# Stick-breaking attention: both heads of a chunk in one instruction on ScalarE, VectorE and GpSimd, and the diagonal closed in the scores

## What is computed

```python
z = jnp.einsum("bhtd,bhsd->bhts", qb, kb) * scale
causal = s_idx < t_idx
log_not = jnp.where(causal, jax.nn.log_sigmoid(-z), 0.0)
tail = lax.cumsum(log_not, axis=3, reverse=True) - log_not
log_a = jax.nn.log_sigmoid(z) + tail
a = jnp.where(causal, jnp.exp(log_a), 0.0)
outs.append(jnp.einsum("bhts,bhsd->bhtd", a, vb))
```

## Time and profile before

| | before |
|---|---|
| median of 3 runs | 2425.4 us (2420.01 to 2426.77) |
| the profiled execution's own time | 2425.43 us |
| its span, first to last instruction | 2423.6 us |
| PE busy | 2293.8 us, 95% |
| DVE, ACT, POOL busy | 959.4, 843.0, 975.7 us |
| granted TensorE clock, mean | 0.955 of full speed |

### The profile page before, as it was taken

One profiled execution on the slowest core, in us unless ns is written; L12 is line 12 of the kernel. 1 busy time (PEld: TensorE's weight loads), 2 busy tenths in 40 slices (PEclk: granted clock), 3 DMA queues, 4 the chain that ended last, 5 costly groups with the idle time before them and its releaser, 6 DMA issues.

```text
span 2423.6 us, 28293 instructions
## 1 busy us (share of the span) xinstructions
PE 2293.8 (95%) x10366; PEld 1801.5 (74%) x10366; DVE 959.4 (40%) x1433; ACT 843.0 (35%) x1410; POOL 975.7 (40%) x435
## 2 busy tenths in 40 slices
PE   7999999998889899999997999999999879999997
PEld 5888887775446688888784888888877547888886
DVE  3121347257663511244754321134523652212245
ACT  4222235325652422223523332222433752322222
POOL 4444444551002544444552354444344313444442
PEclk9999999999888999999997999999998879999999
DMA  4222222331001223223231132222231001322221
GB/s 162 104 92 99 104 104 87 122 121 36 1 1 52 85 89 104 87 104 107 85 111 45 70 105 103 93 97 103 70 104 70 1 1 70 104 88 102 97 93 70
DMA packets 29801, 202.67 MB, mean 84 GB/s; under 512 B 3360, under 2 KB 4000, under 8 KB 6048
## 3 DMA queue, kind: packets, MB, share of 16 engines
q1 hardware_dynamic: 28800, 198.55, 23.3%
q10 hardware_dynamic: 928, 3.14, 0.4%
HBM read 198.54 MB, written 2.10 MB: 83 GB/s over the span
## 4 chain that ended last, share of the span: by engine, by line
PE 86%; DVE 6%; ACT 4%; issue 2%; POOL 1%; DMA 1%; ACTq 0%; SPq 0%; DVEq 0%; POOLq 0%
PE PS L879 26%; PE PS L881 26%; PE PS L880 26%; PE PS L1185 2%; PE PS L1154 2%; PE PS L1113 1%; DVE NMAX L1558 1%; PE PS L1286 1%; DVE ACC L1344 1%; PE PS L1274 1%; ACT PT L677 1%; DVE TMP L1424 1%; PE PS L948 1%; DMA RAW<-wstream 1%; POOL X L437 1%
## 5 line engine op out<-in xcount | busy, mean ns | idle before, releaser
L412 POOL TENSOR_TENSOR WL<-RAW,WH 128x1024 fp32r<-128x1024 f32 x368 | 909.5, 2474 | 1335.3 <-ACT WH L478 1335.3
L879 PE MATMUL PS<-XH,WH 128*128 128x512 f32 (+1 forms) x2200 | 867.6, 394 | 29.9 <-DVE XL L1336 23.3
L880 PE MATMUL PS<-XL,WH 128*128 128x512 f32 (+1 forms) x2200 | 856.6, 389 | 0.0
L881 PE MATMUL PS<-XH,WL 128*128 128x512 f32 (+1 forms) x2200 | 856.1, 389 | 0.0
L478 ACT ACTIVATE WH<-RAW 128x1024 fp32r<-128x1024 f32 x368 | 388.6, 1060 | 1293.1 <-PE PS L881 1255.4
L879 PEld LDWEIGHTS PS<-XH,WH 128*128 128x128 f32 x2200 | 417.7, 190 | 126.1 <-issue 26.7
L880 PEld LDWEIGHTS PS<-XL,WH 128*128 128x128 f32 x2200 | 417.8, 190 | 87.9 <-issue 4.1
L881 PEld LDWEIGHTS PS<-XH,WL 128*128 128x128 f32 x2200 | 417.5, 190 | 85.7
L879 PE MATMUL PS<-HH,WH 128*128 128x512 f32 x672 | 261.4, 389 | 0.0
L880 PE MATMUL PS<-HL,WH 128*128 128x512 f32 x672 | 261.4, 389 | 0.0
L881 PE MATMUL PS<-HH,WL 128*128 128x512 f32 x672 | 261.4, 389 | 0.0
(11 more groups left out here) (193 smaller groups left out, 1667.5 us busy)
## 6 DMA issues: line engine op xcount, KB each, us to landing
RAW<-wstream SPq DMA_DIRECT2D x183, 1024.0 KB, 4.8
X<-xT SPq DMA_DIRECT2D x4, 512.0 KB, 9.6
WORK<-memT ACTq DMA_DIRECT2D x2, 1024.0 KB, 5.3
outT<-WORK SPq DMA_DIRECT2D x8, 256.0 KB, 2.1
RAW<-wstream SPq DMA_DIRECT2D x2, 512.0 KB, 6.8
PB<-WORK ACTq DMA_DIRECT2D x8, 127.8 KB, 2.4
CST<-consts SPq DMA_DIRECT2D x1, 912.0 KB, 11.6
WORK<-constsb SPq DMA_DIRECT2D x1, 256.0 KB, 13.2
```

The source lines that it names most:

```text
L412: pool.tensor_tensor(WL[:, s, :, :].rearrange("p a b -> p (a b)"), RAW[:, s, :], WH[:, s, :, :].rearrange("p a b -> p (a b)").bitcast(F), ...
L879: pe.matmul(o, wh, xh, start=start, stop=False)
L880: pe.matmul(o, wh, xl, start=False, stop=False)
L881: return pe.matmul(o, wl, xh, start=False, stop=stop)
```

## The change

Steps become pairs: `SBPAIRS` lists 24 of (chunk, key tile), and each operation of ACT, DVE and POOL takes both heads of a pair in one instruction, over a tile of two rows. The lags are 2 and 3, in pairs. The slots are grouped in twos; L goes to one of two slots of a pair (half of PB, and a new tile LT). The diagonal's bf16 matmul moves from the end of the tail to behind the scores, ahead of clip; DVE's mask multiplication is gone. The tails of both heads wait for the one subtraction of their pair, and the weights for both tails.

```diff
-LAG_T = 4
-LAG_V = 6
-SBANKS = 6
+LAG_T = 2
+LAG_V = 3
...
+        LT = sb("LT", [P, 2, S])
...
-        ASLOT = [PB[:, 2, :], PB[:, 3, :], W[:, 20, :], W[:, 21, :]]
-        ESLOT = [PT[:, 0, :], PT[:, 1, :], TMP[:, 0, :], TMP[:, 1, :]]
+        ASLOT = [PB[:, 2:4, :], W[:, 20:22, :]]
+        ESLOT = [PT[:, 0:2, :], TMP[:, 0:2, :]]
+        LSLOT = [PB[:, 0:2, :], LT[:, :, :]]
+        def sb_bank(p):
+            return slice(2 * (p % 3), 2 * (p % 3) + 2)
+        def sb_x(p):
+            return slice(2 * (p % 4), 2 * (p % 4) + 2)
...
-        SBSTEPS = [(2 * c + r, j) for c in range(6) for j in range(NT - 1, -1, -1) for r in range(2)]
+        SBPAIRS = [(c, j) for c in range(6) for j in range(NT - 1, -1, -1)]
...
-                for t, (h, j) in enumerate(SBSTEPS):
+                for p, (c, j) in enumerate(SBPAIRS):
                     w = S - j * P
-                    pool.wait_ge(sb_hi, t + 1)
-                    pool.tensor_tensor(XL[:, t % 8, 0:w], PB[:, t % 2, 0:w], XH[:, t % 8, 0:w].bitcast(F),
+                    pool.wait_ge(sb_hi, p + 1)
+                    pool.tensor_tensor(XL[:, sb_x(p), 0:w], LSLOT[p % 2][:, :, 0:w], XH[:, sb_x(p), 0:w].bitcast(F),
                                        ALU.subtract).then_inc(sb_lo, 1)
...
+            def sb_exp_ln(p):
+
+                e = ESLOT[p % 2][:, :, 0:S - SBPAIRS[p][1] * P]
+                act.wait_ge(sb_clip, p + 1)
                 act.activation(e, e, ACT.Exp).then_inc(sb_exp, 1)
-                act.wait_ge(sb_exp, t + 1)
+                act.wait_ge(sb_exp, p + 1)
                 act.activation(e, e, ACT.Ln, bias=1.0).then_inc(sb_ln, 1)
...
+            def sb_round(p):
+
+                w = S - SBPAIRS[p][1] * P
+                act.wait_ge(sb_l, p + 1)
+                if p >= 4:
+                    act.wait_ge(sb_tri, 2 * p)
+                act.activation(XH[:, sb_x(p), 0:w], LSLOT[p % 2][:, :, 0:w], ACT.Copy).then_inc(sb_hi, 1)
+
+            def sb_weights(p):
+                w = S - SBPAIRS[p][1] * P
+                act.wait_ge(sb_tri, 2 * p + 2)
+                if p >= 2:
+                    act.wait_ge(sb_pv, 2 * p - 2)
+                act.activation(ASLOT[p % 2][:, :, 0:w], PS[:, sb_bank(p), 0:w], ACT.Exp).then_inc(sb_a, 1)
+
+            for p in range(n + LAG_T):
+                if p >= LAG_T:
+                    sb_weights(p - LAG_T)
+                if p < n:
+                    sb_exp_ln(p)
+                if 1 <= p <= n:
+                    sb_round(p - 1)
...
+            def sb_scores(p):
+                c, j = SBPAIRS[p]
+                if p >= 3:
+                    pe.wait_ge(sb_a, p - 2)
+                for r in range(2):
+                    f = slice(DH * r, DH * r + DH)
+                    pe.matmul(PS[:, 2 * (p % 3) + r, 0:S - j * P], W[f, 8 + c, j * P:(j + 1) * P],
+                              Q[f, c, j * P:S], start=True, stop=False, skip_group_check=True)
+                for r in range(2):
+                    pe.matmul(PS[:, 2 * (p % 3) + r, 0:P], IDB, CSB[:, B_STRICT:B_STRICT + P], start=False,
+                              stop=False, skip_group_check=True).then_inc(sb_qk, 1)
+
+            def sb_tail(p):
+
+                c, j = SBPAIRS[p]
                 w = S - j * P
+                pe.wait_ge(sb_lo, p + 1)
+                for r in range(2):
+                    bank = PS[:, 2 * (p % 3) + r, :]
+                    for n in range(NT - j):
+                        col, width, m = n * P, w - n * P, SUMS[:, 1 if n == 0 else 0, :]
+                        for part in (XH, XL):
+                            mm = pe.matmul(bank[:, col:w], m, part[:, 2 * ((p - n) % 4) + r, 0:width], start=False,
+                                           stop=n == NT - j - 1 and part is XL, skip_group_check=True)
+                    mm.then_inc(sb_tri, 1)
...
             pe.wait_ge(sums_ready, 1)
+            for p in range(n + LAG_V):
+                if p < n:
+                    sb_scores(p)
+                if 0 <= p - LAG_T < n:
+                    sb_tail(p - LAG_T)
+                if p >= LAG_V:
+                    sb_values(p - LAG_V)
             pe.wait_ge(sb_o, 6)
...
+            def sb_clip_(p):
+                w = S - SBPAIRS[p][1] * P
+                dve.wait_ge(sb_qk, 2 * p + 2)
+                if p >= 2:
+                    dve.wait_ge(sb_l, p - 1)
+                dve.tensor_scalar(ESLOT[p % 2][:, :, 0:w], PS[:, sb_bank(p), 0:w], SPW, None,
                                   ALU.min).then_inc(sb_clip, 1)
...
-                chain(dve.tensor_tensor(lt[:, 0:w], ESLOT[t % 4][:, 0:w], PS[:, t % SBANKS, 0:w], ALU.max))
-                dve.tensor_tensor(lt[:, 0:P], lt[:, 0:P], CST[:, K_MASK:K_MASK + P], ALU.mult).then_inc(sb_l, 1)
...
+            def sb_soft(p):
+
+                w = S - SBPAIRS[p][1] * P
+                dve.wait_ge(sb_ln, p + 1)
+                if p >= 2:
+                    dve.wait_ge(sb_lo, p - 1)
+                lt = LSLOT[p % 2]
+                dve.tensor_tensor(lt[:, :, 0:w], ESLOT[p % 2][:, :, 0:w], PS[:, sb_bank(p), 0:w],
+                                  ALU.max).then_inc(sb_l, 1)
```

More of the change, by code:

```diff
@@ L829, in _ @@
             project("projB")
[L830 to L834, removed]
+            n = len(SBPAIRS)
+            def sb_exp_ln(p):
+                e = ESLOT[p % 2][:, :, 0:S - SBPAIRS[p][1] * P]
+                act.wait_ge(sb_clip, p + 1)
                 act.activation(e, e, ACT.Exp).then_inc(sb_exp, 1)
-                act.wait_ge(sb_exp, t + 1)
+                act.wait_ge(sb_exp, p + 1)
                 act.activation(e, e, ACT.Ln, bias=1.0).then_inc(sb_ln, 1)
[L839 to L860, removed]
+            def sb_round(p):
[17 more added lines that the diff above has]
+                    sb_round(p - 1)
             round_o(range(5), lambda k: act.wait_ge(sb_o, k + 1))
@@ L1265, in _ @@
             pe.wait_ge(turned, FLIPS[max(FLIPS)]["c"])
[L1267 to L1279, removed]
-                w = S - j * P
[L1281 to L1289, removed]
@@ L1291, in sb_values @@
-            def sb_values(t):
-                h, j = SBSTEPS[t]
-                c = h // 2
+            n = len(SBPAIRS)
+            def sb_scores(p):
[9 more added lines that the diff above has]
+                              stop=False, skip_group_check=True).then_inc(sb_qk, 1)
@@ L1294, in sb_values @@
+            def sb_values(p):
+                c, j = SBPAIRS[p]
                 w = S - j * P
-                pe.wait_ge(sb_a, t + 1)
-                if h % 2 == 0 and j == NT - 1 and c >= 2:
+                pe.wait_ge(sb_a, p + 1)
+                if j == NT - 1 and c >= 2:
                     pe.wait_ge(sb_o, c - 1)
-                r = slice(DH * (h % 2), DH * (h % 2) + DH)
-                pe.matmul(PS[r, 6 + c % 2, j * P:S], V_SB[:, j, h * DH:(h + 1) * DH], ASLOT[t % 4][:, 0:w],
-                          start=j == NT - 1, stop=j == 0, skip_group_check=True).then_inc(sb_pv, 1)
@@ L1302, in _ @@
-            pe.wait_ge(sums_ready, 1)
[L1303 to L1313, removed]
+                for r in range(2):
+                    f, h = slice(DH * r, DH * r + DH), 2 * c + r
+                    pe.matmul(PS[f, 6 + c % 2, j * P:S], V_SB[:, j, h * DH:(h + 1) * DH],
+                              ASLOT[p % 2][:, r, 0:w], start=j == NT - 1, stop=j == 0,
+                              skip_group_check=True).then_inc(sb_pv, 1)
@@ L1669, in _ @@
             project("projB", "kv")
-            n = len(SBSTEPS)
+            n = len(SBPAIRS)
             def sb_take(c):
@@ L1674, in sb_take @@
                 dve.tensor_copy(W[:, c, :], PS[:, 6 + c % 2, :]).then_inc(sb_o, 1)
[L1676 to L1681, removed]
-                                  ALU.min).then_inc(sb_clip, 1)
[L1684 to L1690, removed]
-                chain(dve.tensor_tensor(lt[:, 0:w], ESLOT[t % 4][:, 0:w], PS[:, t % SBANKS, 0:w], ALU.max))
-                dve.tensor_tensor(lt[:, 0:P], lt[:, 0:P], CST[:, K_MASK:K_MASK + P], ALU.mult).then_inc(sb_l, 1)
[L1694 to L1701, removed]
+            def sb_clip_(p):
[4 more added lines that the diff above has]
+                dve.tensor_scalar(ESLOT[p % 2][:, :, 0:w], PS[:, sb_bank(p), 0:w], SPW, None,
+                                  ALU.min).then_inc(sb_clip, 1)
+            def sb_soft(p):
[6 more added lines that the diff above has]
+                                  ALU.max).then_inc(sb_l, 1)
+            for p in range(n + LAG_V + 2):
+                if p < n:
+                    sb_clip_(p)
+                if 1 <= p <= n:
+                    sb_soft(p - 1)
+                d = p - LAG_V - 1
+                if 0 <= d < n and d % 4 == 3:
+                    sb_take(d // 4)
             low_o("outB", range(5))
```

## The result

The changed kernel takes 2476.4 us (median of 4 runs, 2475.4 to 2480.9) against 2422.7 us before (4 runs): 53.7 us more. The measured ratio is 1.0232, with a 95% interval of 1.0207 to 1.0257 (the ratios here are those on record and differ by up to 0.2% from the quotient of the two medians). It is slower. The forecast was 2485 us with a range of 2460 to 2499, so the time lies in the range, 9 us under the forecast. The profiled execution took 2475.35 us, with a span of 2473.6 us.

The account below looks back on a forecast made before the run. An ACT–PE loop paced the stick-breaking stage; merging makes one serial chain. A 24.6 us upper-clock chunk plus 0.65 × 5.2 gives 28.0; six plus ends make 172.5 against 112.4, so 2425.4 + 60 = 2485 us, range 2460 to 2499.

Parts of the forecast that it names:

- The order: ACT's list: rounding directly before its pair's weights, so ACT waits out POOL and PE in all 24 pairs, 2 to 8 us.
- The durations: Stick-breaking stage: merged instructions cost one fixed part plus twice the elements; ACT 11.55 us a chunk, POOL 6.19.
- DVE at nothing: Stick-breaking stage: losing 48 mask multiplications (26.9 us busy) on DVE gains no time, being off the chain.
- the chunk at the upper clock: Stick-breaking chunk, PE at full clock: ACT 11.55, POOL 6.19, tails 6.04, hand-overs 0.8, together 24.6 us.
- hand-overs and drain: Between engines, per pair: 0.10 us PE to ACT, 0.06 each for the other two, drain 0.16.
- The clock's term: PE's tails partly at the lower clock: 0.65 × 5.2 us added per chunk, 24.6 becoming 28.0 us.
- share of two thirds: Stick-breaking stage: part of PE's tail work assumed to run at the lower clock level, taken as 0.65.
- two bounds: Stick-breaking stage: clock at the upper level throughout, +39 us, or at the lower level throughout, +71 us.
- the rule gave 2496 us: Rival in the stage: same chain, PE's clock down throughout, +65 to +71 us, 2490 to 2496; chance 0.25.
- The faster one: Rival in the stage: fewer fixed parts and no DVE masks pay, 10 us less, 2415 us; chance 0.04.
- The clock mostly up: Rival in the stage: same chain with PE's clock mostly upper, +39 to +46 us, 2464 to 2471; chance 0.2.

Follow-up runs that it names:

- filler run: Changed kernel with 7 to 28 further matmuls of 256 columns on PE ahead of each pair's scores, their output overwritten; 2466.5 us, ratio 1.0175.
- the diagonal alone: Kernel before, in single steps, with only the diagonal's bf16 matmul moved behind the scores and DVE's mask multiplication dropped; 2418.0 us, ratio 0.9998.
- the pairs alone: Changed kernel with the diagonal as before: bf16 matmul at the end of each tail, two DVE mask multiplications per pair; 2483.7 us, ratio 1.0283.

## Why the prediction was right

**The order.** That the rounding stands directly before its weights was the whole argument, and it held: 24 of 24 weights wait, for 1.6 us in the narrowest pairs (9.3 us over 6) and up to 7.5 us in the widest, where 2 to 8 us were forecast (the narrowest lie just under). Taking the rounding behind the weights gave 27.7 us of the stage, and the same order without merging cost 38 us.

**The durations.** ACT's pairs sum to 11.56 us a chunk (Exp 2.91, Ln 2.95, rounding 2.88, weights 2.82), where 11.55 was worked out; POOL's to 6.14 against 6.19 (the prediction's own formula gives 0.73 for its narrowest pass, where it wrote 0.76). DVE is busy for 41.6 us, forecast at 44.

**DVE at nothing** was right: without its masks alone the time of the kernel before does not move (0.9998), and in the changed kernel ACT waits 1.2 us for DVE in the whole stage.

**The term that was mis-sized** is the chunk at the upper clock, put at 24.6 us. The filler run shows 24.16 at a clock of 0.99. The excess is in the tails and their hand-overs: from the end of POOL's pass to the weights the four pairs of a chunk take 0.75 + 1.23 + 1.94 + 2.85 = 6.8 us there, where 6.04 for the tails and 4 × (0.06 + 0.10 + 0.16) for hand-overs and drain make 7.3. The hand-over from PE to ACT alone is 0.04 us (1956.59 to 1956.63), not 0.10.

**The clock's term** held: taken were 0.65 of a possible 5.2 us a chunk, so 3.4 us. In the changed kernel the tails of key tiles 3 and 2 run at the upper level (0.75 and 1.23 us as above, with one exception at 2.06 in the first chunk), those of key tile 1 at the lower level (3.34 us instead of 1.94), and those of key tile 0 mostly at the lower level (4.65 us on average instead of 2.85: some 4.3 and some 4.9 to 5.0, in turn). This is 3.2 us a chunk, a share of 0.62. The granted clock during the tails of tile 0 in one chunk, and of tiles 3, 1 and 0 in the next:

```profile
1934.64:1938.87 4.23, 4.23 (x18) 3.83 (x20) 0.00 (x0) 0.00 (x0) 0.00 (x0) 0.61 0.00 0
1942.27:1942.94 0.67, 0.67 (x6) 0.60 (x8) 0.44 (x1) 0.00 (x0) 0.00 (x0) 1.00 0.00 0
1953.35:1956.59 3.24, 3.24 (x14) 3.12 (x15) 0.00 (x0) 0.00 (x0) 0.00 (x0) 0.50 0.00 0
1961.62:1966.49 4.87, 4.87 (x18) 4.41 (x20) 0.00 (x0) 0.00 (x0) 0.00 (x0) 0.52 0.00 0
```

So the picture that the prediction gave (the long tails of tile 0 lift the clock each time) is what the trace shows: the tails of tile 3 behind them run at 1.00. But the share of two thirds was a choice between two bounds and not worked out; that it came within 0.2 us is in part luck. The expectation of the filler run took 2.6 us for this term, by subtracting the forecast's 24.6 from the measured 27.2; with the measured 24.16 it is 3.0 to 3.2. In six chunks the upper-clock term makes some 2.7 us and the clock's term 1.2, and the stage came out 4.2 us under the 172.5 of the forecast. The trace agrees in part with the Trainium skill ("TensorE: Matmul & The Clock Gate", section "HAM oscillation — how this bites in real kernels"), by which pauses between bursts bring the clock down each time. The tails of tiles 3 and 2 follow pauses too and run at 1.00. In each chunk the clock falls between the tails of tile 2 and those of tile 1 (at about 1949.4 us, while PE works on scores ahead of its longest pause in this chunk); in every other chunk it also rises ahead of the tails of tile 0 and falls again within them. The stage has a mean of 0.71, between the 0.50 by which the rule gave 2496 us and 1.00.

**What was not in the sum** lies outside the stage. From the stage's last copy to the end of the program the kernel before took 454.8 us and the changed one 450.2, with the same instructions. The clock differs there too:

```profile
1968.80:2013.80 45.00, 35.53 (x130) 19.90 (x131) 19.86 (x60) 16.07 (x46) 0.90 (x1) 0.58 0.00 1
```

is the memory attention of the kernel before, and the same 45 us of the changed kernel and of the diagonal alone are

```profile
2023.40:2068.40 45.00, 35.61 (x155) 21.62 (x156) 20.45 (x60) 17.06 (x47) 3.44 (x2) 0.77 0.07 23
```

```profile
1967.40:2012.40 45.00, 35.55 (x174) 23.39 (x175) 20.51 (x61) 18.13 (x48) 4.79 (x2) 0.89 0.06 24
```

with a clock of 0.58, 0.77 and 0.89, and 454.8, 450.2 and 445.0 us to the end of the program. It does not follow the change: the pairs alone, merged like the changed kernel, have 0.62 and 454.3 us. So 60 forecast stand against 55.9 in the stage and 53.7 in the medians; the forecast's base of 2425.4 us was also 2.7 above the median of 2422.7 that the changed kernel was measured against.

**The rivals.** The faster one needed a wait of at most 1.2 us a pair; it is 99.3 / 24 = 4.1. The clock mostly up is what the filler brought about by force, and 2466.5 us lies within the 2464 to 2471 given to it. The Trainium skill's advice to minimise the count of chained operations on VectorE ("VectorE: DVE Perf Modes", section "Rules for kernel authors") bought nothing in this stage: the diagonal alone takes DVE from 151 instructions to 103 at a ratio of 0.9998, since DVE was not what the others waited for.

## What to carry to other kernels

Before merging instructions, write out the list of the engine that is waited for and look at what stands between an instruction and the one that depends on it through other engines: with the lags kept equal in steps, merging two heads left nothing between rounding and weights where the work of two whole steps had stood, and the wait it exposed (4.1 us a pair) was far more than the fixed parts saved (0.1 to 0.2 us an instruction). If fixed parts or the wait between two dependent instructions hurt, put the two heads' single instructions side by side instead: that kept the overlap and, with the diagonal moved as well, made the stage 22% shorter. In a chain over several engines, a lag should be counted in pieces of work between the two ends, not in loop steps.

## What the runs showed of the hardware that was not expected

More work on PE made the stage faster: some 340 matmuls whose result is overwritten took it from 168.3 to 152.2 us, with the granted clock going from 0.71 to 0.96. In the other direction, an order that leaves PE few pauses gains twice, by the pause and by the clock: 111.8 us at 0.83 became 96.2 us at 0.96 and 87.5 us at 0.98, with the same 480 matmul records. And the memory attention behind the stage, with the same instructions in every kernel here, ran at mean clocks of 0.58 to 0.89 in its first 45 us. The time from the stage's end to the program's falls into three groups in the thirteen profiles: 454.1 to 454.8 us in nine (clock 0.58 in one, 0.62 in eight), 450.2 or 450.3 in three (0.77) and 445.0 in one (0.89). What decides between these three was not tried; it is a spread of 10 us that single profiles of this program carry.
